# Second mixer of a two-model transformer kernel: attention and recurrence issued between the projections' matmuls

## The chip, the cores and the metric

The kernel runs on one core of a Trainium2 chip. TensorE (PE) does matrix products, its weight loads are listed apart (PEld); VectorE (DVE), ScalarE (ACT) and GpSimd (POOL) do elementwise work; SyncE (SP) issues most DMAs. Each engine runs its own instruction list in order and waits on semaphores. The metric is the device time of one execution, in microseconds (us).

## What is computed

Two models in a row, 512 tokens of width 1024, all in float32. In feature-major form an activation is 8 chunks of 128 features by 512 tokens. The order is: gated feed-forward, mixer (attention and pooling), gated feed-forward, final norm; then twice a mixer and a convolutional feed-forward. The change is in the first mixer of the second model, the `even_mixer` of the reference:

```python
def even_mixer(y, w_in, w_out, sinks, lb, gnorm_w):
    proj = y @ w_in                       # 1024 -> 2816: q, k, v, then q, f, i, g of HGRN
    qa, ka, va, qb, fb, ib, gb = jnp.split(proj, EVEN_SPLITS, axis=-1)
    # 8 query heads of 64 on 2 key heads, rotary; chunk attention over 128 tokens back, with sinks
    oa = chunk_band_attention(qa, ka, va, A_PREV_CHUNKS, None, sinks)
    ob = hgrn2(qb, fb, ib, gb, lb, gnorm_w)            # 4 heads, key and value width 128
    return jnp.concatenate([oa, ob], axis=-1) @ w_out

# hgrn2, over 16 blocks of 32 tokens: f = lb + (1 - lb) sigmoid(fb), k = 1 - f, cum = cumsum(log f)
#   q_dec = q exp(cum), k_dec = k exp(-cum), k_end = k exp(last - cum)
#   o_intra = causal(q_dec k_dec^T) v ;  o_inter = q_dec state
#   state   = exp(last) state + k_end^T v
#   o = rms_norm over the head's 128 values, times norm_w, times silu(gb)
```

## The kernel before

The network is a list `STAGES`: `up1 down1 in1 out1 up2 down2 in2 out2 up3 down3 in3 out3 up4 down4`. A product of a 128x128 weight tile with 512 tokens is done by `product` as three matmuls (high part times high part, high times low, low times high: L1135 to L1137), since each operand is split in a rounded part and a rest. I call these three a tile product. `in2` has 22 output chunks of 8 tile products (176), `out2` has 64.

Weights come in pairs of 16 tiles (1 MB) through two slots. SP loads `raw`, ACT rounds to `w_hi`, DVE subtracts to `w_lo` and releases the pair (`lo_rounded`), PE waits for that semaphore at the pair's start. In plain stages this is one 128x2048 instruction on each engine (L1337, L1370); in woven stages it is cut in four 128x512 pieces (`round_piece` L1352, `rest_piece` L1360), issued at every fourth tile product of the pair before; the last piece of a pair stands on DVE two tile products after it stands on ACT.

Two kinds of mixer code exist. `in1/out1` and `in3/out3` are woven: one loop over tile products g = 1, 2, ... on PE, ACT and DVE, and at fixed g each engine also issues a slot of attention (in `in1/out1` every third g). `in2/out2` is not woven. Its `in2` runs a pair at a time, with the two chunks of a pair interleaved, so that each chunk of the input `x_split` serves two tile products in a row; `hgrn_prepare_act` and `hgrn_prepare_dve` are called between pairs, and two `hgrn_transpose` stand between pairs on PE. Then `attention_pe/act/dve` run (8 heads by 4 query blocks, 32 units), then `hgrn_pe/act/dve` (4 heads), and then `out2`. In the HGRN part the output is made feature by token, so the sum of squares over a head's features is a matmul with ones (`mean_square`, L858), and the inverse root comes back through another (`spread_root`, L863). Its recurrence is 15 DVE instructions in a chain per head (L1043).

At the start of `in2`, ACT and DVE still make `x_split` chunk by chunk from the final norm of the first model (L1394, L1398), and PE waits for chunk k before it uses it. `mix_hi` and `mix_lo` are the split input of `out2`. `hg_kend` and the like are semaphores of the HGRN part.

## Time and profile before

| | us |
|---|---|
| median of 3 runs | 2252.61 |
| lowest and highest of them | 2243.70, 2253.09 |
| profiled execution | 2243.01 |
| its span in the trace | 2241.2 |
| PE busy in it | 2188.5 |
| DVE busy | 1169.6 |
| ACT busy | 716.9 |
| from the first tile product of in2 (901.48) to the end of out2's last (1199.34) | 297.86 |

PE is busy for 98% of the span by the page, but a busy PE is not a PE at full speed: a matmul's end is modelled, and the granted clock counts. The times between the starts of neighbouring matmuls tell more. DVE and ACT are far from full over the whole run; in a stage whose steps depend on them they may still be late.

### The profile page before, as it was taken

To read this page: it belongs to the slowest core of one execution; us is meant where nothing else is said; L and a number is where in the kernel's file an instruction comes from. 1 tells how busy PE (TensorE), PEld (TensorE's weight loads), DVE (VectorE), ACT (ScalarE), POOL (GpSimd) and SP (SyncE) were. 2 spreads that over 40 slices of the span, in tenths; PEclk is the share of its full clock that TensorE was granted. 3 is DMA by queue.
4 is the path that set the end of the run, shared out by engine and by line. 5 is a ranking of instruction groups with operands and counts; after the bars stand their busy time and mean duration, and the time that the engine had idled before them with its cause. 6 is when DMAs were issued, how large, how long until landed. Compare 5 with 4: busy or idle time off the path is not lost.

```text
span 2241.2 us, 26561 instructions
## 1 busy us (share of the span) xinstructions
PE 2188.5 (98%) x10146; PEld 1754.0 (78%) x10146; DVE 1169.6 (52%) x1777; ACT 716.9 (32%) x1012; POOL 119.7 (5%) x111
## 2 busy tenths in 40 slices
PE   8999999999999999999999999999899999999997
PEld 6888888677888888785687888888677777888886
DVE  4444434776444433744656666632655557666523
ACT  4222222354222222532313322222444444232221
POOL 0000000400000000000002000000411102000001
PEclk9999999999999999997979999999999999999998
DMA  7222234112222233221002222223222212222231
GB/s 251 94 98 106 68 103 155 62 43 90 98 106 96 71 100 123 81 94 57 1 11 69 91 100 106 77 89 113 79 75 95 76 60 80 105 94 94 77 103 64
DMA packets 32880, 198.99 MB, mean 89 GB/s; under 512 B 3760, under 2 KB 4064, under 8 KB 16048
## 3 DMA queue, kind: packets, MB, share of 16 engines
q1 hardware_dynamic: 29664, 184.91, 23.8%
q0 software_dynamic: 2992, 12.97, 2.0%
q8 instruction: 40, 0.66, 0.1%
q10 hardware_dynamic: 160, 0.26, 0.0%
q14 instruction: 24, 0.20, 0.0%
HBM read 195.74 MB, written 7.38 MB: 91 GB/s over the span
## 4 chain that ended last, share of the span: by engine, by line
PE 93%; DVE 3%; POOL 1%; ACT 1%; issue 1%; DMA 0%; POOLq 0%; SPq 0%; DVEq 0%; ACTq 0%
PE ps L1135 28%; PE ps L1136 27%; PE ps L1137 27%; POOL h L1815 1%; PE ps L633 1%; PE ps L651 1%; PE ps L1115 1%; PE ps L430 1%; PE ps L899 1%; PE ps L622 1%; PE ps L450 1%; PE ps L742 1%; PE ps L1131 1%; PE ps L756 0%; ACT w_hi L1337 0%
## 5 line engine op out<-in xcount | busy, mean ns | idle before, releaser
L1135 PE MATMUL ps<-x_split,w_hi 128*128 128x512 f32 x1856 | 738.4, 398 | 19.5 <-DVE x_split L1398 13.7
L1136 PE MATMUL ps<-x_split,w_hi 128*128 128x512 f32 x1856 | 724.8, 391 | 0.0
L1137 PE MATMUL ps<-x_split,w_lo 128*128 128x512 f32 x1856 | 724.7, 390 | 0.0
L1337 ACT ACTIVATE w_hi<-raw 128x2048 fp32r<-128x2048 f32 (+2 forms) x169 | 289.2, 1711 | 602.5 <-PE ps L1137 597.2
L1370 DVE TENSOR_TENSOR w_lo<-raw,w_hi 128x2048 fp32r<-128x2048 f32 (+2 forms) x169 | 344.3, 2037 | 219.3 <-ACT w_hi L1337 218.8
L1135 PEld LDWEIGHTS ps<-x_split,w_hi 128*128 128x128 f32 x1856 | 349.5, 188 | 111.1 <-DVE x_split L1398 14.2
L1136 PEld LDWEIGHTS ps<-x_split,w_hi 128*128 128x128 f32 x1856 | 349.8, 188 | 73.3 <-issue 3.6
L1137 PEld LDWEIGHTS ps<-x_split,w_lo 128*128 128x128 f32 x1856 | 349.5, 188 | 73.7
L1135 PE MATMUL ps<-act,w_hi 128*128 128x512 f32 x896 | 353.5, 395 | 1.6 <-DVE w_lo L1360 1.5
L1137 PE MATMUL ps<-act,w_lo 128*128 128x512 f32 x896 | 349.7, 390 | 0.0
L1136 PE MATMUL ps<-act,w_hi 128*128 128x512 f32 x896 | 349.7, 390 | 0.0
L1135 PEld LDWEIGHTS ps<-act,w_hi 128*128 128x128 f32 x896 | 168.8, 188 | 41.4 <-issue 4.4
L1137 PEld LDWEIGHTS ps<-act,w_lo 128*128 128x128 f32 x896 | 168.6, 188 | 35.6
L1136 PEld LDWEIGHTS ps<-act,w_hi 128*128 128x128 f32 x896 | 168.8, 188 | 35.0 <-issue 0.8
L1694 DVE TENSOR_TENSOR gate<-ps,rstd 128x512 f32<-128x512 f32 x44 | 30.4, 691 | 174.2 <-PE ps L1137 174.2
L1514 ACT ACTIVATE act<-prod 128x512 f32 (+1 forms) x88 | 55.6, 632 | 202.4 <-DVE prod L1714 202.4
L1738 DVE TENSOR_TENSOR act<-prod,act 128x512 f32 (+1 forms) x88 | 60.9, 692 | 88.3 <-ACT act L1514 88.3
L1697 DVE TENSOR_TENSOR shifted<-ps,rstd 128x512 f32<-128x512 f32 x44 | 30.4, 692 | 105.4 <-PE ps L1137 105.3
L1496 ACT ACTIVATE gated<-gate 128x512 f32<-128x512 f32 x88 | 54.8, 623 | 93.1 <-DVE gate L1709 85.9
L1815 POOL TENSOR_TENSOR h<-h,gate 128x512 f32<-128x512 f32 x16 | 24.6, 1535 | 1116.4 <-DVE gate L1771 1116.4
L1360 DVE TENSOR_TENSOR w_lo<-raw,w_hi 128x512 fp32r<-128x512 f32 x92 | 68.9, 753 | 26.9 <-ACT w_hi L1352 26.7
L1374 ACT ACTIVATE sq<-y 128x512 f32<-128x512 f32 (+1 forms) x32 | 19.8, 631 | 149.8 <-DVE y L1728 143.9
(224 smaller groups left out, 1679.6 us busy)
## 6 DMA issues: line engine op xcount, KB each, us to landing
raw<-in_w_up SPq DMA_DIRECT2D x88, 1024.0 KB, 4.8
raw<-in_w_in SPq DMA_DIRECT2D x28, 1024.0 KB, 4.8
raw<-in_w_down SPq DMA_DIRECT2D x32, 768.0 KB, 4.2
raw<-in_w_down SPq DMA_DIRECT2D x32, 640.0 KB, 3.8
raw<-in_w_out SPq DMA_DIRECT2D x12, 1024.0 KB, 4.8
skew<-scratch POOLq DMA_DIRECT2D x1, 5120.0 KB, 30.4
biases<-skew POOLq DMA_DIRECT2D x16, 256.0 KB, 3.0
h<-in_x_t SPq DMA_DIRECT2D x4, 512.0 KB, 10.2
```

The source lines that it names most:

```text
L1135: pe.matmul(bank(b), hi, rhs_hi, start=start, stop=False)
L1136: pe.matmul(bank(b), hi, rhs_lo, start=False, stop=False)
L1137: return pe.matmul(bank(b), lo, rhs_hi, start=False, stop=stop)
L1337: eng.activation(w_hi[:, w], raw[:, w], ACT.Copy).then_inc(hi_rounded, 1)
L1360: ins = eng.tensor_tensor(w_lo[:, w], raw[:, w], w_hi[:, w].bitcast(F32), ALU.subtract)
L1370: eng.tensor_tensor(w_lo[:, w], raw[:, w], w_hi[:, w].bitcast(F32), ALU.subtract).then_inc(lo_rounded, 1)
L1496: eng.activation(gated[:, :], gate[:, :], ACT.Silu if st.evac == "silu" else ACT.Gelu)\
L1514: eng.activation(chunk(act, f), prod[:, :], ACT.Copy).then_inc(prod_hi, 1)
L1694: eng.tensor_tensor(gate[:, :], bank(b), rstd[:, :], ALU.mult).then_inc(gate_ready, 1)
L1697: eng.tensor_tensor(shifted[:, 2:], bank(b), rstd[:, :], ALU.mult).then_inc(u_ready, 1)
L1738: eng.tensor_tensor(chunk(act, KF + f), prod[:, :], chunk(act, f).bitcast(F32), ALU.subtract)\
L1815: eng.tensor_tensor(chunk(h, m), chunk(h, m), (gate, gated)[m % 2][:, :], ALU.add).then_inc(h_ready, 1)
```

## The change

`in2` and `out2` become woven stages, by the code of `in1/out1`, which now takes the layer number `a` (0 or 1). The 22 output chunks of `in2` are made one at a time ( in the order f, g, then i and q in turns, then key, query, query, value, query, query of attention). The first four chunks have banks of their own, as in `in3`, so that PE needs not wait for the norm's factor `rstd` early.

Attention of this layer uses the grouped code of `in1` (16 steps that take two heads together, every third g from g = 154 on, into `out2`), without the doubled key copy `kdup` and its selection matrices; the swapped key halves come by two DMAs that ACT issues at g = 143. HGRN stands at fixed g: preparation at g = 26 to 70, heads 0 to 3 at a distance of 16 g between g = 70 and 145. Its output is made token by feature: the query part is the stationary operand (32 columns), the state moves (128 columns), the sum of squares comes from ACT's accumulator, and a transpose brings the normed output back. `out2` takes its inputs in the order HGRN first, attention last, the first four of each sum for all eight chunks and then the last four, with `y` added up in two parts on DVE. Weights of `in2/out2` are rounded in pieces.

```diff
-    Stage("in2", "in", 11, 11, "project"), Stage("out2", "in", KD // 2, KD // 2, "hold"),
+    Stage("in2", "in", 11, 22, "weave"), Stage("out2", "in", KD // 2, 2 * KD, "weave_hold", first=4),
-IN2_ORDER = [*range(10, 14), *range(6, 10), *range(18, 22), *range(14, 18), *range(0, 6)]
+IN2_ORDER = [*range(10, 14), *range(18, 22), 14, 6, 15, 7, 16, 8, 17, 9, 4, 0, 1, 5, 2, 3]
...
+        def hgrn_pe(pe, g):
+            hd, e = divmod(g - 64, 2 * KD)
+            if 0 <= hd < 4 and e == 6:
+                pe.wait_ge(hg_kend, 1)
...
+                    ins = pe.transpose(bank(O_BANK)[:, n * P:(n + 1) * P], chunk(hf, hd)[:, n * P:(n + 1) * P], ident)
...
+            if 0 <= hd < 4 and e == 11:
+                pe.wait_ge(evacuated, BY["in2"].g0 + 2 * hd + 9)
+                pe.wait_ge(hg_tb, hd + 1)
+                if hd:
+                    pe.wait_ge(hg_on, hd)
...
+            if 0 <= hd < 4 and e == 14:
+                pe.wait_ge(hg_ta, hd + 1)
...
+                    ins = pe.matmul(bank(UPDATE_BANKS[r])[:, n * P:(n + 1) * P], hf[rows, w], hv[rows, w], start=True, stop=True)
...
+            hd, e = divmod(g - 80, 2 * KD)
+            if 0 <= hd < 4 and e == 3:
+                pe.wait_ge(hg_q, hd + 1)
...
+            if 0 <= hd < 4 and e == 8:
                 pe.wait_ge(hg_s, hd + 1)
+                pe.wait_ge(hg_state, (NHB - 1) * (hd + 1))
...
+                            ins = pe.matmul(bank(O_BANK)[32 * r:32 * r + 32, n * P:(n + 1) * P],
+                                            chunk(hq, hd)[:, b * HGRN_BLOCK:(b + 1) * HGRN_BLOCK], state[hd % 2][:, state_col(b)],
+                                            start=False, stop=True, skip_group_check=True)
                 ins.then_inc(hg_o, 1)
...
+            if 0 <= hd < 4 and e == 13:
+                pe.wait_ge(hg_on, hd + 1)
...
+        def hgrn_act(eng, g):
...
+            if g == 43:
                 eng.wait_ge(hg_f, 2)
                 eng.activation(hf, hf, ACT.Ln).then_inc(hg_ln, 1)
+            if g == 59:
+                eng.wait_ge(hg_cum, 1)
+                eng.activation(he[:, :], hc[:, :], ACT.Exp).then_inc(hg_exp, 1)
                 eng.wait_ge(hg_diff, 1)
                 eng.activation(hf, hf, ACT.Exp).then_inc(hg_exp, 1)
+                eng.wait_ge(hg_exp, 1)
                 eng.activation(hc[:, :], hc[:, :], ACT.Exp, scale=-1.0).then_inc(hg_exp, 1)
...
+            hd, e = divmod(g - 80, 2 * KD)
+            if 0 <= hd < 4 and e == 9:
                 eng.wait_ge(hg_o, hd + 1)
+                for n in range(NB):
+                    w = slice(n * P, (n + 1) * P)
+                    ins = eng.activation(o_sq[:, w], bank(O_BANK)[:, w], ACT.Square, accum_out=h_sum[:, n:n + 1])
+                ins.then_inc(hg_osq, 1)
+                eng.wait_ge(hg_osq, hd + 1)
+                eng.activation(h_std, h_sum, ACT.Sqrt, bias=lbs[:, 31:32], scale=1.0 / P).then_inc(hg_std, 1)
...
+        def hgrn_dve(eng, g, link):
...
+            for hd in range(4):
+                at_ = 64 + 2 * KD * hd
+                if g in (at_ + 15, at_ + 17):
...
+                    for b in range(8) if g == at_ + 15 else range(8, NHB - 1):
...
+            hd, e = divmod(g - 80, 2 * KD)
+            if 0 <= hd < 4 and e == 0:
+                eng.wait_ge(evacuated, BY["in2"].g0 + 2 * hd + 10)
+                eng.tensor_tensor(chunk(hq, hd), chunk(hq, hd), chunk(he, hd), ALU.mult).then_inc(hg_q, 1)
...
+            if 0 <= hd < 4 and e == 11:
+                eng.wait_ge(hg_std, hd + 1)
+                link(eng.reciprocal(h_inv, h_std))
...
-            def in1_pe(pe, st):
+            def weave_pe(pe, st, a):
+                end = KD * st.groups
+                own = {2: TURN_BANK, 3: TURN_BANK + 1} if a else {}
+                mean_at, spread_at = ((6, 9), (2 * KD + 2, 3 * KD))[a]
...
+                    if a == 1:
+                        hgrn_pe(pe, g)
```

What stands in a row on ACT, where the exponentials of the preparation are. `w_hi<-raw` is the rounding of weights, `hc` holds the running sums, `he` their exponentials. Before:

```order
L921 ACT_TABLE_LOAD
L921 ACTIVATE proj<-proj 128x2048 [waits hg_diff]
L922 ACTIVATE he<-hc 128x2048
L924 ACTIVATE hc<-hc 128x2048 [waits hg_exp]
L1337 ACTIVATE w_hi<-raw 128x2048 [waits pair_done,raw_landed1]
```

After (g = 48 to 68):

```order
L1156 ACTIVATE w_hi<-raw 128x512 [waits pair_done,raw_landed1]
L1156 ACTIVATE w_hi<-raw 128x512 x2
L745 ACT_TABLE_LOAD
L745 ACTIVATE he<-hc 128x2048 [waits hg_cum]
L747 ACTIVATE proj<-proj 128x2048 [waits hg_diff]
L749 ACTIVATE hc<-hc 128x2048 [waits hg_exp]
L1156 ACTIVATE w_hi<-raw 128x512
L1156 ACTIVATE w_hi<-raw 128x512 [waits pair_done,raw_landed0]
L752 ACT_TABLE_LOAD
L752 ACTIVATE proj<-proj 128x2048 [waits evacuated]
```

The fourth piece of a pair's rounding, which the tile product g = 65 needs, now stands behind the three exponentials.

On PE, the recurrent part of one HGRN head, before (L889 and L899 make the output of head 0, then the updates of head 1 and the sum of squares):

```order
L868 MATMUL ps<-proj,hc 128x128 x4
L899 MATMUL ps<-proj,state_98 128x32 [waits hg_state] x15
L876 MATMUL ps<-proj 128x128 x15
L858 MATMUL ps<-small,osq 128x1 [waits hg_osq]
L858 MATMUL ps<-small,osq 128x1 x3
```

After, from g = 88 to 93 (L951 to L953 are the tile product):

```order
L716 MATMUL ps<-proj,sq 128x128 [waits hg_tb,hg_state,hg_s]
L716 MATMUL ps<-proj,sq 128x128 x3
L722 MATMUL ps<-state_88,proj 32x128 x15
L951 MATMUL ps<-x_split,w_hi 128x512 [waits evacuated]
...
L688 MATMUL ps<-small,proj 128x128 [waits hg_on,hg_tb,evacuated]
L688 MATMUL ps<-small,proj 128x128 x3
...
L729 MATMUL ps<-small,gate 128x128 [waits hg_on]
L729 MATMUL ps<-small,gate 128x128 x3
```

There are three tile products between the head's output (L722) and the transposes (L688), which wait for the normed output of this head, and two more before L729.

On DVE, the same head, before and after (`w_lo<-raw` is the weight rest; L1400 takes a projection chunk out of PSUM):

```order
L1040 COPY state0_98<-ps 128x128 [waits hg_u_ps]
L1043 SCALAR_TENSOR_TENSOR state0_98<-state0_98,tiny_66,ps 128x128 [waits hg_state] x14
L1005 COPY_PREDICATED s_t_100<-mconst_68,ps 128x512 [waits hg_s_ps]
```

```order
L832 COPY state0_88<-ps 128x128 [waits hg_u_ps]
L835 SCALAR_TENSOR_TENSOR state0_88<-state0_88,tiny_66,ps 128x128 [waits hg_state] x7
L1400 TENSOR_TENSOR proj_67<-ps,rstd_62 128x512 [waits pair_done]
L840 TENSOR_TENSOR proj_67<-proj_67,he_86 128x512 [waits evacuated]
L835 SCALAR_TENSOR_TENSOR state0_88<-state0_88,tiny_66,ps 128x128 [waits hg_state] x7
L1164 TENSOR_TENSOR w_lo_54<-raw_52,w_hi_53 128x512 [waits hi_piece]
L848 COPY_PREDICATED sq_60<-mconst_68,ps 128x512 [waits hg_s_ps,const_landed]
```

The chain of states is now cut in two, with a chunk's eviction and the query product (L840) between the halves.

## Rows read from the trace of the kernel before

**Rows 1.** Windows (start:end length, busy of PE, PEld, DVE, ACT, POOL, PEclk, DMA, GB/s).

```profile
901.48:1029.46 127.98, 125.95 (x572) 103.66 (x571) 72.45 (x67) 49.40 (x42) 0.00 (x0) 1.00 0.25 91
1029.46:1103.76 74.30, 66.29 (x252) 35.46 (x253) 46.13 (x183) 31.56 (x103) 0.00 (x0) 0.82 0.04 15
1103.76:1153.00 49.24, 46.82 (x344) 42.34 (x345) 35.59 (x85) 6.33 (x12) 0.00 (x0) 0.70 0.00 1
1153.00:1199.34 46.34, 46.34 (x194) 37.75 (x193) 18.21 (x20) 9.52 (x10) 0.00 (x0) 0.95 0.20 68
```

**Rows 2.** Timeline of PE in out2 (start, us, instruction).

```profile
1159.20 0.39 PE L1135 MATMUL ps<-act,w_hi 128*128 128x512 f32 x1
1159.43 0.40 PE L1136 MATMUL ps<-act,w_hi 128*128 128x512 f32 x1
```

**Rows 3.** Timeline of PE, one attention slot of in1.

```profile
444.30 0.82 PE L730 MATMUL ps<-small,g_exps 128*128 128x128 f32 x6
445.04 0.48 PE L742 MATMUL ps<-proj 64*128 64x256 f32 x1
...
445.68 0.88 PE L756 MATMUL ps<-g_turned,g_vtok 128*64 128x128 f32 x12
446.48 0.50 PE L1135 MATMUL ps<-x_split,w_hi 128*128 128x512 f32 x1
446.82 0.39 PE L1136 MATMUL ps<-x_split,w_hi 128*128 128x512 f32 x1
```

**Rows 4.** Timeline of PE, one rotary slot of in1.

```profile
452.34 1.02 PE L815 MATMUL ps<-proj,mconst 128*128 128x512 f32 x2
452.80 0.80 PE L1135 MATMUL ps<-x_split,w_hi 128*128 128x512 f32 x1
```

**Rows 5.** Timeline of PE, transposes and first HGRN products of in2.

```profile
970.01 1.91 PE L848 MATMUL ps<-small,proj 128*128 128x128 f32 x16
971.67 0.48 PE L1135 MATMUL ps<-x_split,w_hi 128*128 128x512 f32 x1
...
1103.76 1.16 PE L868 MATMUL ps<-proj,hc 128*128 128x128 f32 x8 [1.41 <-DVE act L531]
1104.85 1.17 PE L876 MATMUL ps<-proj 32*128 32x128 f32 x30
1105.94 1.16 PE L889 MATMUL ps<-s_t,proj 128*128 128x128 f32 x8
```

**Rows 6.** Timeline of DVE: last chunk of x_split before in2.

```profile
909.70 0.75 DVE L1398 SCALAR_TENSOR_TENSOR x_split<-h,vec,x_split 128x512 fp32r<-128x512 f32 x1 [0.38 <-ACT x_split L1394]
```

**Rows 7.** Timeline of ACT in in2.

```profile
929.24 1.28 ACT L915 ACT_TABLE_LOAD   x1
930.53 1.92 ACT L915 ACTIVATE hk<-proj 128x2048 f32<-128x2048 f32 x1
```

**Rows 8.** Groups of DVE, 905 to 1203.3 (count | busy us, mean ns | idle before).

```profile
L1043 DVE SCALAR_TENSOR_TENSOR state<-state,tiny,ps 128x128 f32<-128x128 f32 x56 | 19.5, 348 | 1.9
L975 DVE TENSOR_TENSOR_SCAN hc<-reset,proj 128x512 f32<-128x512 f32 x4 | 4.6, 1206 | 0.9 <-ACT proj L918 0.9
L979 DVE TENSOR_TENSOR proj<-hc 128x2048 f32<-128x2048 f32 x1 | 2.3, 2292 | 0.0
```

**Rows 9.** Groups of DVE, weight pieces in in1 and out1.

```profile
L1360 DVE TENSOR_TENSOR w_lo<-raw,w_hi 128x512 fp32r<-128x512 f32 x32 | 27.1, 853 | 3.4 <-ACT w_hi L1352 3.4
```

**Rows 10.** Groups of ACT, 905 to 1203.3.

```profile
L478 ACT ACTIVATE near<-near,tiny 128x129 f32<-128x129 f32 x4 | 1.6, 403 | 6.8 <-DVE tiny L524 6.8
L478 ACT ACTIVATION_READ_ACCUMULATOR near<-near,tiny 128x1 f32 x18 | 3.4, 188 | 0.0
```

**Rows 11.** Windows: PE thinly used, with its clock.

```profile
403.00:409.00 6.00, 4.83 (x19) 3.12 (x18) 5.97 (x6) 1.84 (x3) 5.59 (x5) 1.00 0.14 30
1040.00:1066.00 26.00, 26.00 (x66) 12.95 (x64) 12.30 (x59) 8.96 (x32) 0.00 (x0) 0.50 0.00 0
1592.00:1600.00 8.00, 5.82 (x18) 4.37 (x19) 7.02 (x7) 4.39 (x7) 3.58 (x4) 0.79 0.17 44
```

760 lines of the change are left out of this document (272 added, 488 removed).

## The prediction

> **What bounds the kernel now.** I read the windows of the stretch that the change touches first, then the starts of neighbouring matmuls on PE, then who waits for whom. Over the whole run PE never rests long, and nearly all of its time is weight tile products. At full clock two matmuls start 0.23 us apart (1159.20, 1159.43) [rows 2], so a tile product of three costs 0.683 us. In the stretch from the first tile product of in2 to the end of out2's last, 901.48 to 1199.34 or 297.86 us, there are 240 of them, which is 163.9 us. The rest, 134 us, is work of another kind, and the windows say where it lies [rows 1]: in2 takes 127.98 for 176 tile products (120.2), so it is almost tight; attention takes 74.30 us and HGRN 49.24 us in which no tile product runs, at a mean clock of 0.82 and 0.70; out2 takes 46.34 for 43.7, since its first tile products run at half clock. In the two middle windows DVE is busy 62% and 72% and ACT 42% and 13%. So neither is full there: PE, DVE and ACT wait for each other in chains of small steps, and the halved clock makes PE's small steps long. What PE does in these 123.5 us is little work. That is what a weave can hide.
>
> **PE's work in the new stretch.** (1) 240 tile products, 163.9 us. (2) Statistics of the norm, as now: two small groups and the tile product after each, about 1.9 us, the same before. (3) Attention: 16 steps. A slot of in1 shows the parts [rows 3]: six transposes take 0.74 (444.30 to 445.04), scores of 256 keys for two heads 0.64 (to 445.68), twelve value passes 0.80 (to 446.48), and the next matmul comes 0.34 instead of 0.23 after the first, which is 0.11 for coming back. With this layer's window a step reads two key blocks (four transposes, eight passes, 256 keys: 0.49 + 0.64 + 0.53 + 0.11 = 1.8), and in the first query block of each of the four head pairs one (about 1.05, with 0.4 taken for scores of 128). 12 x 1.8 + 4 x 1.05 = 25.8 us; say 26. (4) Five rotary products: 0.46 each (452.34 to 452.80), and the first matmul after one is 0.80 long where 0.39 is usual, so 0.9 each, 4.5 us [rows 4]. The transposes of v: 0.5. (5) HGRN, per head: three groups of four transposes at 1.66 / 4 = 0.42 (970.01 to 971.67 for sixteen), scores 1.09, updates 1.09, the part within a block about 1.0 [rows 5], and the part with the state. This last has no row: before, the state was the stationary operand and 32 columns moved; now 32 columns are stationary and 128 move, with 15 products in four groups of array columns. The nearest rows are the updates, which use a quarter of the rows each and take 1.09 for 30 passes [rows 5], and the value passes of attention, which use half of the columns by turns and take 0.067 each, so 2.0 for 30 [rows 3]. Without any overlap it would be 1.09 / 8 = 0.136 for a pass, 4.1 us for 30. I take 1.1, since four groups follow one another as in the updates; the other end adds 3.0 x 4 = 12 us. A head is 3 x 0.42 + 1.09 + 1.09 + 1.0 + 1.1 = 5.5, with six returns at 0.11 it is 6.2, four heads 24.8 us. Together PE has 163.9 + 1.9 + 26 + 4.5 + 0.5 + 24.8 = 221.6 us of work at full clock.
>
> The Trainium skill (TensorEngine Tiling (Array Packing), Key Properties) says that changing the tiling mode drains TensorE, which speaks against small matmuls strewn among large ones. It gives no time. The slot above holds such changes in both directions and its 2.18 us include them, so the sum would be the same by the rule.
>
> **PE's waits in the new stretch.** These I follow through the order of each engine, with g for the tile product at which a step stands.
>
> - Start. PE waits for input chunk k before tile product k. In the old order a chunk served two tile products, now one, so PE runs up to the producer. DVE ends the eighth chunk at 910.45 (909.70 + 0.75) [rows 6], and g = 8 ends at 911.2 where it would end at 906.9: 4.3 us lost.
> - g = 33. DVE waits for the norm's factor, then does four weight pieces, three evictions and four tiny steps, 4 x 0.75 to 0.85 + 3 x 0.69 + 0.9 = 6.2 or more from some 0.6 + 0.7 after PE's spread; PE needs the fourth piece after 0.4 + 8 x 0.683 = 5.9. About 1.3 us [rows 9].
> - g = 65. The preparation is a chain: sigmoid on ACT, f and k on DVE (3.4, four of 128x512 at 0.54 and one of 128x2048 at 1.23 in the same view as rows 8), logarithm on ACT, four scans on DVE (1.21 each), difference (2.29), exponentials on ACT; a 2048-wide step on ACT is 1.92 and a table load ahead of it 1.28 [rows 7, 8]. From the end of g = 32 at 929.5 I get: sigmoid done 933.5, f and k 937.1, logarithm 939.1, scans 948.2 with three weight pieces and an eviction among them, difference 952.1 (two more in front), exponentials 950.2, 954.1, 956.0. The fourth piece of the rounding stands behind them on ACT, 956.7, and its rest on DVE ends at 957.5. PE has finished g = 64 at 952.6 and waits 4.8 us. Queued behind that wait on PE is everything; on DVE the eviction of g = 64 and k_end.
> - Each head, g = +3: the query product on DVE stands behind eight state steps (2.9 with 0.35 each and small gaps [rows 8]), and an eviction. PE reaches the scores 2.05 us after it finished the pair, the product is there after 3.1. 1.0 us each, 4 us.
> - Each head, g = +11: after the head's output ACT squares four blocks with the accumulator. The nearest rows are exponentials of 129 columns, 0.40 + 0.19 for the read [rows 10], 2.4 us for four; then root 0.26, DVE reciprocal and product 0.9, with semaphores 3.7. PE has three tile products to do, 2.05 us, before the next head's transposes wait for this. 1.65 us for three heads, 5 us, and 1.3 once for the table load of the root [rows 7]. The last head has no such transposes.
> - Attention. The slots of in1 follow each other at 4.3 us for wider steps with hardly a gap, and DVE's load per slot is smaller here; 1 us.
>
> That is 4.3 + 1.3 + 4.8 + 4 + 5 + 1.3 + 1 = 21.7 us. DVE in a head has about 13 us of work in 20, so it is not the bound; ACT less. Weight pieces take DVE 4 x 0.75 for a pair where one instruction took 2.29, hidden in that slack, save at the three places above. SP's loads move nothing: 1 MB per pair, released at the same tile product as now. The constants' DMA of POOL is 3/4 as long and lands before g = 100. The end of out2 with its norm is as in out3, a few tenths either way.
>
> **The clock.** At half clock a tile product costs twice. In3 starts with the same hunger for input chunks, and its window 1592 to 1600 has a clock of 0.79: 1.7 us at half, 0.9 us lost. At 403 to 409 PE was busy 80% with a gap of 1.2, and the clock stayed at 1.00. From 1040 to 1066, after gaps and with thin work, it was 0.50 throughout [rows 11]. After the wait at g = 65 the clock may fall and come back under dense work, as in out2, whose window is 2.6 us over its 43.7 [rows 1]. I take 2.5 us for both.
>
> ACT's table loads: in the trace the work after a load begins at once, 929.24 + 1.28 against 930.53 [rows 7]. The Trainium skill (ScalarE: Activation LUTs, What ACT_TABLE_LOAD costs) gives about 1.38 us of drain on top of 1.28. By that rule the chain to g = 65 would be 2 x 1.38 longer, and the sum 3 us higher; the trace does not agree, and I leave it out.
>
> **The sum.** 221.6 + 21.7 + 2.5 = 245.8 us against 297.9, a gain of 52.1 us. On the profiled execution's own time, 2243.0, this gives 2190.9. The median of the three runs is 2252.6, which is 9.6 above the profiled execution; one of the three ran like it, 2243.7. I carry the same distance over: 2200 us, about 2.3% faster.
>
> **Rivals.**
> (a) PE's work and fewer waits: the chains at g = +3 and +11 are shorter than I count (squares at 0.35 each), and the wait at g = 65 is half as long. Gain 60 to 68, 2185 to 2193. For it: in1 and out1 have almost no waits on PE. Against: HGRN's chain has three more engine changes for a head than attention's.
> (b) Longer waits or slower state products: no overlap of the column groups (+12), or the clock falls at each head's waits and half of the HGRN stretch of some 78 us runs at half level, which adds 0.9 us (0.68 and the small work with it) for each of about 25 of its g, 20 us. Gain 20 to 40, 2213 to 2233. For it: HGRN before ran at 0.70. Against: there PE had only small matmuls, and here 11 of 20 us are dense.
> (c) Slower than before: the clock, once fallen at g = 65, stays at half to the end of the weave, because the waits of every head keep PE too thin, as in 1040 to 1066 [rows 11]. Each g from 65 on then costs 0.68 and its small work again, about 0.9 us. From some 58 g's on (52 / 0.9) the gain is gone; the 111 that remain of in2 with the part of out2 up to its slots would cost 100, 2300 us. Against it: out2 came back to full clock within about 5 us of tile products alone. The Trainium skill (TensorE: Matmul & The Clock Gate, HAM oscillation) tells of a kernel whose waits bring the clock down again and again; here the rows with a gap of 1.2 us show none.
> (d) The weave doesn't do what it says, since a semaphore makes PE stand at the first HGRN slot until the preparation is over and the rest runs as before: the order gives PE tile products on both sides of each slot, so only a small chance; no change, 2252.
>
> **Chances.** The forecast 0.55 (2193 to 2208), (a) 0.17, (b) 0.23, (c) 0.03, (d) 0.02. The likeliest time is 2200. The range leaves out (c), (d) and the far part of (b): 2183 to 2224. A measurement of this kernel tells about 0.5% (11 us) from no change; faster by more has 0.96, within it 0.02, slower by more 0.02.
>
> **What would show it.** In the profile after: no stretch without tile products between in2 and out2; the two starts 246 us apart (235 to 270); on PE a wait for `w_lo` of about 5 us some 56 us after in2's start; a wait for `x_split` at the start of 4 us in small parts; waits of 1 to 2 us for `gate` (the normed output) three times, and four of about 1 us for the query product; the state products at 1.1 us for 30 passes; the clock near 1.00 everywhere but at the start and after g = 65. The forecast is wrong if the clock row shows half level across the heads, if the state products take 4 us, or if DVE is busy without a break in the heads, which would mean that its chains and not PE's work set the pace.

## The result and the profile after

The changed kernel takes 2185.24 us (median of 4 runs, 2185.03 to 2185.57) where the kernel before takes 2252.85 (4 runs, 2243.70 to 2260.18). The ratio is 0.9719, interval 0.9685 to 0.9753. The forecast was 2200 in a range of 2183 to 2224, so the direction and the range hold; the time lies 2 us above the range's low end, below the forecast's own 2193 to 2208 and at the fast end of rival (a), 2185 to 2193. In the groups of runs below, two of the 27 runs of the kernel before took 3223.7 and 3113.4 us at a mean granted clock of 0.63 and 0.65; the ratios leave them out.

The page of the profiled execution (2185.57 us) shows PE where it was in share, with less time in all, and no slice at a low clock:

```profile
span 2183.6 us, 26539 instructions
PE 2132.3 (98%) x10116; PEld 1709.3 (78%) x10116; DVE 1164.7 (53%) x1810; ACT 726.3 (33%) x1071; POOL 119.9 (5%) x111
PEclk9999999999999999999999999999999999999999
```

The stretch from in2's first tile product to the end of out2's last takes 239.77 us (902.39 to 1142.16) where it took 297.86. Outside the stretch next to nothing moved: 1943.34 us before, 1943.83 after. The windows (start:end length, busy of PE, PEld, DVE, ACT, POOL, PEclk, DMA, GB/s) are the whole stretch, the piece after the wait at g = 65, and the HGRN heads:

```profile
902.39:1142.16 239.77, 227.99 (x1331) 173.70 (x1329) 167.53 (x389) 105.39 (x225) 0.00 (x0) 0.99 0.18 63
956.45:962.28 5.83, 5.83 (x19) 4.57 (x20) 5.80 (x6) 3.47 (x3) 0.00 (x0) 0.71 0.56 183
962.28:1041.60 79.32, 73.88 (x569) 58.66 (x567) 51.66 (x112) 23.54 (x66) 0.00 (x0) 1.00 0.16 54
```

The two windows at clocks 0.82 and 0.70 [rows 1] have no counterpart. The heads now share 79.32 us with 71 tile products at full clock, and DVE is busy 65% of it: its load doesn't set the pace there, but the order of its steps still makes PE wait, as the next lines show.

What PE still waits for in the stretch, but for one wait of 0.2 us (engine, line waited for: us in total, times, longest):

```profile
PE ps L951 <- DVE w_lo L1164: 3.8, 2, 3.4
PE ps L707 <- DVE proj L840: 3.1, 4, 0.8
PE ps L688 <- DVE gate L855: 2.4, 3, 1.6
PE ps L951 <- DVE x_split L1202: 2.2, 6, 0.8
```

These are the four kinds that the prediction named: the weight piece at g = 65, the query product, the normed output, and the input chunks. The timeline rows (start, us, instruction, idle before it) show each. First PE at g = 64 and 65, then a row after it, then ACT and DVE beside it:

```profile
952.70 0.39 PE L953 MATMUL ps<-x_split,w_lo 128*128 128x512 f32 x1
956.45 0.50 PE L951 MATMUL ps<-x_split,w_hi 128*128 128x512 f32 x1 [3.36 <-DVE w_lo L1164]
...
959.31 0.63 PE L951 MATMUL ps<-x_split,w_hi 128*128 128x512 f32 x1
959.74 0.63 PE L952 MATMUL ps<-x_split,w_hi 128*128 128x512 f32 x1
```

```profile
953.26 1.89 ACT L749 ACTIVATE hc<-hc 128x2048 f32<-128x2048 f32 x1
955.06 1.13 ACT L1156 ACTIVATE w_hi<-raw 128x512 fp32r<-128x512 f32 x2
```

```profile
955.70 0.69 DVE L1164 TENSOR_TENSOR w_lo<-raw,w_hi 128x512 fp32r<-128x512 f32 x1 [3.69 <-ACT w_hi L1156]
```

ACT's weight piece stands behind its exponentials, the last of which ends at 955.15; DVE's piece waits for it, and PE for DVE. From 958.03 to 961.02 matmuls start 0.43 apart (959.31 to 959.74) where it is 0.23 at full clock. The granted clock is at its half level from 957.83 to 961.25, 3.4 us, and that costs 1.7 us against the full level.

Then PE in the first head:

```profile
974.36 1.16 PE L707 MATMUL ps<-proj,hc 128*128 128x128 f32 x8 [0.78 <-DVE proj L840]
...
979.27 1.05 PE L716 MATMUL ps<-proj,sq 128*128 128x128 f32 x8
980.25 1.07 PE L722 MATMUL ps<-state,proj 128*32 128x128 f32 x30
981.25 0.50 PE L951 MATMUL ps<-x_split,w_hi 128*128 128x512 f32 x1
...
985.22 0.63 PE L688 MATMUL ps<-small,proj 128*128 128x128 f32 x4 [1.64 <-DVE gate L855]
```

And ACT behind the output (981.25 on):

```profile
981.38 0.28 ACT L765 ACTIVATE prod<-ps 128x128 f32<-128x128 f32 x1 [2.19 <-PE ps L722]
981.55 0.19 ACT L765 ACTIVATION_READ_ACCUMULATOR prod<-ps 128x1 f32 x1
...
982.54 1.28 ACT L768 ACT_TABLE_LOAD   x1
983.84 0.30 ACT L768 ACTIVATE tiny<-tiny,lbs 128x4 f32<-128x4 f32 x1
```

The 15 state products, 30 passes on PE, take 1.00 us (980.25 to 981.25), near the forecast's value of 1.1 and not at its other end. The four squares with their reads take 1.16 us (981.38 to 982.54), not 2.4: the next square follows after 0.25 to 0.27 us, since a square and its read overlap.

### The profile page after: what moved, and what is told of

It is laid out like the page before. It is cut to its first block, busy times and chain, and to the rows that moved or that the text cites. A ratio compares the mean times of both kernels' runs of the same rounds, so it can differ in the third digit from the quotient of the medians.

```text
span 2183.6 us, 26539 instructions
## 1 busy us (share of the span) xinstructions
PE 2132.3 (98%) x10116; PEld 1709.3 (78%) x10116; DVE 1164.7 (53%) x1810; ACT 726.3 (33%) x1071; POOL 119.9 (5%) x111
## 4 chain that ended last, share of the span: by engine, by line
PE 92%; DVE 4%; ACT 2%; POOL 1%; issue 1%; DMA 0%; POOLq 0%; SPq 0%; DVEq 0%
PE ps L951 28%; PE ps L953 27%; PE ps L952 27%; POOL h L1629 1%; PE ps L449 1%; PE ps L467 1%; PE ps L565 1%; PE ps L931 1%; PE ps L579 1%; PE ps L438 1%; PE ps L553 1%; ACT x_split L1198 1%; DVE w_lo L1164 1%; PE ps L947 1%; ACT w_hi L1141 1%
## 5 line engine op out<-in xcount | busy, mean ns | idle before, releaser
L951 PE MATMUL ps<-x_split,w_hi 128*128 128x512 f32 x1856 | 744.4, 401 | 25.3 <-DVE x_split L1202 16.3
L953 PE MATMUL ps<-x_split,w_lo 128*128 128x512 f32 x1856 | 725.9, 391 | 0.0
L951 PEld LDWEIGHTS ps<-x_split,w_hi 128*128 128x128 f32 x1856 | 349.9, 189 | 122.8 <-DVE x_split L1202 19.4
L1141 ACT ACTIVATE w_hi<-raw 128x2048 fp32r<-128x2048 f32 (+2 forms) x155 | 262.4, 1693 | 531.0 <-PE ps L953 522.4
L1174 DVE TENSOR_TENSOR w_lo<-raw,w_hi 128x2048 fp32r<-128x2048 f32 (+2 forms) x155 | 312.3, 2015 | 211.9 <-ACT w_hi L1141 211.5
L953 PEld LDWEIGHTS ps<-x_split,w_lo 128*128 128x128 f32 x1856 | 350.0, 189 | 74.5
L951 PE MATMUL ps<-act,w_hi 128*128 128x512 f32 x896 | 353.4, 394 | 1.8 <-DVE w_lo L1164 1.5
L953 PE MATMUL ps<-act,w_lo 128*128 128x512 f32 x896 | 349.0, 390 | 0.0
L951 PEld LDWEIGHTS ps<-act,w_hi 128*128 128x128 f32 x896 | 168.1, 188 | 43.0 <-issue 6.6
L953 PEld LDWEIGHTS ps<-act,w_lo 128*128 128x128 f32 x896 | 168.2, 188 | 35.6
L1164 DVE TENSOR_TENSOR w_lo<-raw,w_hi 128x512 fp32r<-128x512 f32 x148 | 107.5, 730 | 36.8 <-ACT w_hi L1156 36.5
L1156 ACT ACTIVATE w_hi<-raw 128x512 fp32r<-128x512 f32 x148 | 88.5, 620 | 68.9 <-PE ps L953 68.7
```

The source lines that it names most:

```text
L951: pe.matmul(bank(b), hi, rhs_hi, start=start, stop=False)
L953: return pe.matmul(bank(b), lo, rhs_hi, start=False, stop=stop)
L1141: eng.activation(w_hi[:, w], raw[:, w], ACT.Copy).then_inc(hi_rounded, 1)
L1156: eng.activation(w_hi[:, w], raw[:, w], ACT.Copy).then_inc(hi_piece, 1)
L1164: ins = eng.tensor_tensor(w_lo[:, w], raw[:, w], w_hi[:, w].bitcast(F32), ALU.subtract)
L1174: eng.tensor_tensor(w_lo[:, w], raw[:, w], w_hi[:, w].bitcast(F32), ALU.subtract).then_inc(lo_rounded, 1)
```

## The experiments

Runs of one changed kernel lie up to 7 us apart (e2_start), so for each kernel I give the median and, from its trace, the length of the stretch and the mean clock of the window 930 to 965, which holds the wait at g = 65. Each group of runs had its own runs of the kernel before, with medians of 2246.7, 2251.9 and 2251.0 us; the yardstick `e0_after` and 3, 7 and 8 ran in the second group, 1, 2, 4 and 9 in the first, 5, 6, 10 and 11 in the third. A median can move a little more than its stretch, because short pieces at the half clock outside the stretch also come and go: outside it the profile of the changed kernel has 1943.8 us, those of e0_after, e1_piece, e9_all and e10_best 1942.4, 1942.2, 1941.4 and 1943.2.

| kernel | median, us | stretch, us | clock, 930 to 965 |
|---|---|---|---|
| before | 2252.85 | 297.86 | |
| after | 2185.24 | 239.77 | 0.95 |
| e0_after (the same again) | 2185.16 | 240.88 | 0.90 |
| e1_piece | 2178.73 | 234.47 | 1.00 |
| e2_start | 2186.64 | 241.94 | 0.95 |
| e3_cols | 2190.38 | 244.34 | 0.95 |
| e4_states | 2183.34 | 237.23 | 1.00 |
| e5_late | 2181.23 | 236.32 | 1.00 |
| e6_table | 2183.74 | 239.56 | 0.90 |
| e7_hburst | 2228.09 | 283.24 | 0.90 |
| e8_aburst | 2198.61 | 252.58 | 0.95 |
| e9_all | 2175.70 | 230.54 | 1.00 |
| e10_best | 2175.24 | 230.07 | 1.00 |
| e11_both | 2241.16 | 297.73 | 0.90 |

**The yardstick.**

> The changed kernel itself once more, as the yardstick for the runs beside it. Both theories: 2185 us within 3 us; whether its runs scatter by 0.5 us (as in its first 4) or by several us shows how far single runs may be read.

Its four runs lie between 2184.61 and 2185.37. The stretch is 1.1 us longer than in the first profile, with more of it at the half clock; so a single stretch is good to 1 to 2 us as long as the wait at g = 65 is there (e4_states and e5_late have it and no half clock, 1.6 us less). Where I name less than that, it is read from the places in the trace that the edit touches.

### What the placing is worth

**HGRN in one burst.** The slots are undone, the work is not:

```diff
                     if a == 1:
-                        hgrn_pe(pe, g)
+                    if a == 1 and g == 129:
+                        for gg in range(64, 147):
+                            hgrn_pe(pe, gg)
```

and alike for ACT (steps from g = 67 on) and DVE (from g = 71 on).

> The changed kernel with all TensorE steps of the four HGRN heads, and the ScalarE and VectorE steps from the first state on, in one burst behind the tile product at g = 129, in place of slots between the tile products; the attention slots stay where they are. No computation is left out. Theory (the gain comes from tile products that fill TensorE's waits for ScalarE and VectorE): a head alone is the chain of transposes, copies, updates, 15 state steps of 0.38 us, scores, mask, intra and state products, squares, roots, normalising and transposing back, some 12 to 15 us with 6.2 us of TensorE work in it; 4 heads with little overlap give 4 x 6 = 24 us of waits and in them the half clock for part of it, 2200 to 2215 us, with a scatter between runs as the kernel before has. Rival (the serial stretch of before was slow for its order of heads and its start, and a burst costs next to nothing): under 2192 us.

Measured: 2228.09 us (2227.55 to 2231.07), the stretch 43.5 longer. The direction is the theory's, the size is beyond its upper end, and the scatter is 3.5 us, not that of the kernel before. The burst's window and its first head on PE:

```profile
1004.44:1074.78 70.34, 38.01 (x354) 31.66 (x352) 32.98 (x83) 13.91 (x49) 0.00 (x0) 0.62 0.00 1
```

```profile
1007.13 1.17 PE L698 MATMUL ps<-proj 32*128 32x128 f32 x30 [0.69 <-ACT proj L759]
1011.99 2.08 PE L707 MATMUL ps<-proj,hc 128*128 128x128 f32 x8 [3.69 <-DVE proj L840]
...
1023.50 1.09 PE L688 MATMUL ps<-small,proj 128*128 128x128 f32 x4 [3.89 <-DVE gate L855]
```

Four heads take 70.3 us. PE is idle for 32.3 of them (I had estimated 24 for all waits), behind the chain of states (3.69) and the normalising (3.89) of each head; and it is busy for 38.0 because the clock has fallen to 0.62. In the slots of the changed kernel the same heads take 30 us: 5.4 idle, and 24.6 for the work and for coming back to tile products. So the burst itself costs 40.3 more, 26.9 of idle time and 13.4 of busy time. The other 3.3 are half clock in tile products: 2.2 in those behind the burst and 1.1 at g = 65, where this execution stayed at the half level longer. The half clock stood in the expectation without a price of its own; it is about two fifths of the cost (13.4 and 3.3 of 43.5).

**Attention in one burst.** The 20 slots and the last rotary step stand between in2 and out2:

```diff
             def slot_at(a, g):
+            if a == 1:
+                return -1
...
+                if a == 1:
+                    rope_pe(pe, a, ROPED[a][-1])
+                    for i in range(20):
+                        grouped_pe(pe, a, i)
```

> The changed kernel with the 20 attention slots and the last rotary step of the second layer in one burst between the projection and the output projection, in place of slots between tile products; the HGRN steps stay woven. No computation is left out. Theory (each slot's 1.5 to 1.8 us of products is followed by a wait for exponentials, products and sums on ScalarE and VectorE that only tile products can fill): 20 slots of some 1 us more, 15 to 25 us and the half clock in part of them, 2200 to 2210 us. Rival (slots of neighbouring groups already fill each other's waits): under 2190 us.

Measured: 2198.61 us, the stretch 12.8 longer; a little less than the theory's 15 to 25. The burst:

```profile
1068.56:1111.22 42.66, 31.98 (x236) 17.99 (x235) 30.37 (x151) 27.01 (x85) 0.00 (x0) 0.92 0.07 24
```

PE is busy for 75% of this burst against 54% of the HGRN one, and the clock holds better (0.92 against 0.62). The slots of neighbouring steps fill each other's waits to a good part: what the rival said is half true. So attention gains 12.8 us from its placing and HGRN 43.5.

**Both.**

> The changed kernel with both bursts: the HGRN heads at g = 129 and the attention slots between the projection and the output projection. Nothing of the new code is left out, only the placing between tile products is undone. Single bursts cost 43.5 us (HGRN) and 12.8 us (attention) in the stretch. Theory (the two are independent): 239.8 + 43.5 + 12.8 = 296.1 us in the stretch, 2241 us in all, so that placing alone makes up the change's gain and the rewritten steps add next to nothing. Rival (in the kernel before the two parts follow each other and share the lowered clock, so together they cost more than apart): over 302 us, 2248 us or more. If runs of this one scatter by several us where the changed kernel scatters by 1, the scatter comes from the stretch at the lowered clock.

Measured: 2241.16 us and a stretch of 297.73, with 296.1 and 2241 expected. The two parts add up, and in the profiled stretch the new code without its placing takes what the old one took (297.73 and 297.86). Its median stays 0.5% below that of the kernel before (ratio 0.9953, interval 0.9925 to 0.9982), whose runs scatter upward. The windows, in order: in2 up to the burst, HGRN, the rest of in2, attention with the last rotary step, out2:

```profile
900.34:1001.41 101.07, 95.05 (x399) 75.28 (x398) 60.22 (x86) 42.66 (x56) 0.00 (x0) 0.97 0.24 83
1001.41:1071.90 70.49, 38.16 (x354) 31.82 (x352) 32.98 (x83) 13.93 (x49) 0.00 (x0) 0.64 0.00 1
1071.90:1110.08 38.18, 38.18 (x155) 29.74 (x153) 20.34 (x31) 7.18 (x13) 0.00 (x0) 0.94 0.21 64
1110.08:1154.19 44.11, 34.27 (x235) 19.72 (x234) 30.54 (x151) 27.19 (x85) 0.00 (x0) 0.85 0.07 24
1154.19:1198.07 43.88, 43.88 (x194) 36.35 (x193) 25.03 (x39) 13.20 (x23) 0.00 (x0) 0.99 0.21 72
```

That the sums agree is partly chance. Beside [rows 1], attention in a row takes 44.1 us where the old code took 74.3, and HGRN in a row 70.5 where the old took 49.2: the grouped attention is the better serial code, and the HGRN order, written for slots, the worse one. Between tile products this matters less, for there PE's own time counts and what is left of the waits. Why the old HGRN order is 21 us quicker in a row wasn't tried. Nor was the old attention code placed in slots: the bursts price the placing of the new code, and what placing would give the old one isn't shown.

### The state products

```diff
-                for n in range(NB):
-                    for r in range(4):
+                for r in range(4):
+                    for n in range(NB):
                         b = 4 * n + r
```

> The changed kernel with the HGRN state products ordered by column group first (8 or 7 products of the same 32 columns in a row) and not block by block (next to each other, four products of four different column groups). After the change the 8 intra products and these 30 together take 1.98 us in a slot. Theory (products of different column groups overlap, so that 30 take 1.1 us): in the new order they run one after another at the spacing of an ordinary product of 128 columns (0.11 to 0.14 us), some 4 us a head in place of 1.1, 4 x 3 = 12 us more and a little less where it fills a wait: 2195 to 2198 us. Rival (a product of 32 columns is simply short, 0.036 us, overlap or none): the same 1.98 us and 2185 us.

Measured: 2190.38 us, the stretch 4.6 longer; between the two. The same place as above on PE:

```profile
978.91 1.05 PE L716 MATMUL ps<-proj,sq 128*128 128x128 f32 x8
979.89 2.24 PE L722 MATMUL ps<-state,proj 128*32 128x128 f32 x30
982.07 0.50 PE L951 MATMUL ps<-x_split,w_hi 128*128 128x512 f32 x1
```

The 15 products take 2.18 us in place of 1.00, 1.2 us a head more, 4.7 for four. So the rival (the order doesn't matter) falls. The single records show why the price is not the theory's 3 us a head. These windows count the passes of L722 alone (length, PE busy, passes, clock); first the changed kernel, then e3_cols:

```profile
980.24:980.38 0.14, 0.13 (x4) 1.00 0.00 0
```

```profile
979.88:980.02 0.14, 0.13 (x1) 1.00 0.00 0
```

In the changed kernel four passes on four column groups start within 0.02 us (980.250 to 980.270), and the next four 0.11 later. In e3_cols passes on the same group start 0.11 us apart, as the theory had it; but the next group begins when the one before it is only about halfway (at 980.14, 980.61 and 981.07, where the first group's six passes start from 979.89 to 980.46), so about two groups run side by side. Mean spacing is 0.073 us there and 0.033 in the changed kernel, a factor of 2.2. A case with no overlap at all was not run, so the forecast's other end, 4.1 us a head, is not measured; even the order by groups stays 1.9 below it.

The Trainium skill (TensorE: Matmul & The Clock Gate, Part 3: Packing small matmuls) has products of different column groups run at the same time. By that the order of column groups matters, and the trace agrees: four starts within 0.02 us against one in 0.11.

### The waits, one by one

**The weight piece at g = 65.**

```diff
-            if g == 59:
+            if g == 61:
                 eng.wait_ge(hg_cum, 1)
                 eng.activation(he[:, :], hc[:, :], ACT.Exp).then_inc(hg_exp, 1)
```

> The changed kernel with ScalarE's HGRN exponentials moved two tile products later (from g = 59 to g = 61), so that they stand behind the weight piece that the tile product at g = 65 needs, not ahead of it. In the trace after the change TensorE waits 3.36 us at 956.45 for that piece and then runs at the half clock until 961.4, which costs about 1.7 us more. Theory (the wait at g = 65 is only ScalarE's order, and the half clock follows from it): both go, 3.4 + 1.7 = 5.1 us less than the changed kernel's 2185.2, 2180.1 us. Rival (the exponentials then delay the next thing in the row, the first products of head 0 or the next piece, by as much): the wait turns up behind 962, and the time is 2183 to 2185.5.

Measured: the stretch is 5.3 us shorter (5.1 expected), the median 2178.73, below the 2180.1 expected because this kernel's profile also has 1.6 us less outside the stretch. The wait at g = 65 is gone, nothing took its place (the 0.5 left of `w_lo` is the one at g = 33, and the other rows read as after), and the clock of the window 930 to 965 is 1.00:

```profile
PE ps L951 <- DVE w_lo L1164: 0.5, 1, 0.5
```

```profile
930.00:965.00 35.00, 34.53 (x181) 28.18 (x180) 26.74 (x34) 24.07 (x24) 0.00 (x0) 1.00 0.27 94
```

The same window of the yardstick:

```profile
930.00:965.00 35.00, 31.65 (x129) 25.60 (x128) 24.22 (x30) 22.33 (x21) 0.00 (x0) 0.90 0.26 90
```

Over all profiles, the three with bursts among them: of the ten with the wait of 3.4 us at this place, eight show the half clock after it and two (e4_states, e5_late) don't; of the three without the wait (e1_piece, e9_all, e10_best) none does. So the wait brings the clock down, but not in every execution.

**The start.**

```diff
                     j, k = divmod(g - 1, KD)
+                    if a == 1 and g <= 2 * KD:
+                        k, j = divmod(g - 1, 2)
```

> The changed kernel with the first tile products of the second layer's projection walked in pairs: each of the first contraction chunks serves both column tiles before the next chunk is needed. After the change TensorE waits 3.6 us in all over the first 8 tile products (902.39 to 911.41) because VectorE makes a chunk of x more slowly than TensorE uses it up. Theory (only the rate of chunks is short): two tile products to a chunk give each chunk 1.37 us of work, the gaps go, and the time falls by 3 to 3.6 us to about 2182. Rival (the second tile's weights come later than the x chunks and TensorE waits for them in their place): 2184 to 2187 us.

Measured: 2186.64 us (2182.66 to 2189.27), the stretch 2.2 longer. The time is the rival's, its reason isn't. The gaps for `x_split` are gone, and PE waits 2.69 us once, for something that neither side had named, the sum of squares of the norm:

```profile
917.09 1.84 PE L941 MATMUL ps<-small,ssum 128*128 128x1 f32 x8 [2.69 <-DVE ssum L1197]
```

```profile
909.73 0.75 DVE L1204 SCALAR_TENSOR_TENSOR x_split<-h,vec,x_split 128x512 fp32r<-128x512 f32 x1 [0.38 <-ACT x_split L1200]
910.40 2.29 DVE L1176 TENSOR_TENSOR w_lo<-raw,w_hi 128x2048 fp32r<-128x2048 f32 x1
912.61 3.54 DVE L1195 TENSOR_TENSOR squares<-squares 128x2048 f32<-128x2048 f32 x2
916.25 0.69 DVE L1197 TENSOR_TENSOR ssum<-squares 128x512 f32<-128x512 f32 x1
```

```profile
917.00:925.00 8.00, 7.91 (x25) 6.66 (x26) 2.59 (x8) 3.31 (x6) 0.00 (x0) 0.57 0.01 2
```

DVE works without a break from the chunks through a weight pair and the squares to the sum at 916.94. PE needs this sum at g = 18 in either order. With the gaps it came there 1.2 us after the sum, without them 2.7 before: the start is bound by DVE's list, and the gaps were the cover of a second wait. And one wait of 2.69 can be dearer than six with 2.2 in sum: here the clock falls after it (0.57 from 917 to 925), which it didn't in the changed kernel's start. In e9_all the same wait left it at 1.00, and there the paired start does gain: from the first tile product to the nineteenth 16.5 us, where the changed kernel takes 17.5. So the edit is worth 1.0 us at full clock and loses 2 when the clock falls.

**The query product.**

```diff
-                    for b in range(8) if g == at_ + 15 else range(8, NHB - 1):
+                    for b in range(4) if g == at_ + 15 else range(4, NHB - 1):
```

> The changed kernel with VectorE's chain of HGRN states cut after 4 blocks instead of 8, so that the query product that TensorE's score matmuls need stands four state steps earlier in VectorE's row. After the change each head's score matmuls wait, 3.1 us over the 4 heads, and each slot loses 0.97 us against its own work. Theory (the query product is late only because of the eight state steps ahead of it): the four waits go, 3 to 4 us less, 2181.5 to 2182 us. Rival (the eleven state steps left over delay the states that the state part's matmuls read): a wait on the states turns up in the slot after, and the time is 2184 to 2187 us.

Measured: 2183.34 us, the stretch 2.5 shorter, of which 1.6 is the half clock that this execution hadn't. What is left for the edit is 0.9: the four waits at L707 give back 4.1, the new ones take 3.2. PE's waits from 965 to 1042:

```profile
PE ps L716 <- DVE sq L848: 2.3, 3, 1.1
PE ps L688 <- DVE gate L855: 2.3, 3, 1.6
```

The four waits at L707 are gone, three at L716 stand in their place: the score mask on DVE now comes behind eleven state steps. The rival's kind was right (a later wait), not its object, which it took to be the states. A cut moves the wait along DVE's chain between a head's updates and its intra products.

**The normed output.**

```diff
-            if 0 <= hd < 4 and e == 11:
+            if 0 <= hd < 4 and e == 12:
                 pe.wait_ge(evacuated, BY["in2"].g0 + 2 * hd + 9)
```

(and ACT's copy of v's transposes at 13, not 12)

> The changed kernel with TensorE's transposes of v for the next HGRN head one tile product later, and ScalarE's copy of them one later. Theory (the normed output is late by less than one tile product for heads 2 and 3 and by more for head 1, where the root's table is loaded): the segments lose 0.5, 0.5 and 0.7 us of their waits, the stretch comes to 238.1 us where it was 239.8, the whole to 2183.5. Rival (ScalarE's copy and the updates behind it then come late as well): the waits turn up at the updates, 239.8 us or more.

Measured in two runs: 2181.23 us, the stretch 3.5 shorter, again without the half clock (1.6), so 1.8 for the edit where 1.7 was expected. The waits for the normed output fall from 2.4 us in three to 1.0 in one, as the theory says, and none comes at the updates.

**The root's table.**

```diff
                 eng.activation(hg, hg, ACT.Silu).then_inc(hg_sig, 1)
+                eng.activation(tiny[:, 252:253], lbs[:, 31:32], ACT.Sqrt)
```

> The changed kernel with a square root of one column on ScalarE right after the gate's Silu at g = 66, so that the table of the root is loaded there and not behind the squares of the first head. Theory A (nothing waits for ScalarE at g = 66 to 68): the first head's wait for the normed output shrinks by the load's 1.28 us, 238.5 us in the stretch. Theory B (seen with all edits together: the load holds up a weight piece and an eviction behind it on ScalarE, and TensorE waits 0.7 us for that at v's first transposes): a gain of 0.6 us or less, 239.2 us.

Measured in two runs: 2183.74 us. The waits for the normed output fall from 2.4 to 1.1 us, by the table load's 1.28, as in theory A; the stretch is 1.3 shorter than the yardstick's, which has the same clock of 0.90 in the window 930 to 965, and 0.2 shorter than the first profile's, which has 0.95. So far A. Theory B's wait shows only where the wait at g = 65 is gone, as in the next kernel.

**All together, twice.** The first version combines the five edits above:

> The edits on the waits of the woven stretch together: exponentials behind the weight piece, paired tile products at the start, the state chain cut at 4, the transposes of v in the HGRN part one tile product later (with ScalarE's copy one later), and a square root of one column ahead of time, so that its table is loaded before the first head's squares. Theory (every wait is the order of one engine's row, and none hides another): 5.1 + 3.3 + 3.5 + 1.7 and up to 0.5 more = about 13.5 us less, 2171.5 us. Rival (some of the waits share a cause, and one that goes lengthens the next): 2176 to 2180 us.

Measured: 2175.70 us, the stretch 9.2 shorter, not 13.5: just below the rival's times, 4 above the theory's. The start gave 1.0 of its 3.3 and the cut at 4 gave 0.9 of its 3.5, as above. And the early table load holds up ACT's weight piece, DVE's rest of it starts only at 957.75 after a wait of 2.09, and v's eviction behind that on DVE is late at g = 76:

```profile
959.10 0.66 PE L688 MATMUL ps<-small,proj 128*128 128x128 f32 x4 [0.66 <-DVE proj L1403]
```

The second leaves the start as in the changed kernel, cuts the states at 6 and loads the table at g = 78:

```diff
+            if g == 78:
+                eng.activation(tiny[:, 252:253], lbs[:, 31:32], ACT.Sqrt)
...
-                    for b in range(8) if g == at_ + 15 else range(8, NHB - 1):
+                    for b in range(6) if g == at_ + 15 else range(6, NHB - 1):
```

> A version from what the runs so far showed: the exponentials behind the weight piece, the state chain cut after 6 blocks (after 8 the query product is late by 0.97 us a head, after 4 the mask of the scores by 0.75), the transposes of v one tile product later, and the root's table loaded at g = 78, where ScalarE has nothing pending, not at g = 66, where it held up a weight piece; the start as in the changed kernel. Theory (VectorE's chain between the updates and the intra products is about as long as the tile products beside it, so a cut in the middle leaves some 0.4 us of wait a head): 5.3 + 4 x 0.5 + 1.8 + 2 x 0.5 = 10 us less in the stretch, 229.7 us there and 2175 us in all. Rival (VectorE's load is what counts, and any cut loses the same 0.75 to 1 us a head): 231.7 us, 2177 us.

Measured: 2175.24 us (2175.09 to 2176.20), the stretch 230.07, with 2175 and 229.7 expected. It has the lowest median, 0.966 of the kernel before (interval 0.961 to 0.971) and 10 us below the changed one; e9_all, 0.5 above it with runs from 2173.95 to 2178.26, can't be told from it. This version with the paired start was not run. What PE still waits for in its stretch:

```profile
PE ps L953 <- DVE x_split L1204: 2.2, 6, 0.8
PE ps L716 <- DVE sq L850: 0.6, 1, 0.6
PE ps L953 <- DVE w_lo L1166: 0.5, 1, 0.5
PE ps L953 <- DVE prod L651: 0.2, 1, 0.2
```

## Why the prediction was right, and where it was off

Its chain of reasons holds: the two serial windows were mostly idle time, half clock and small matmuls taken a few at a time, and tile products fill them. The clock alone took 28 of their 123.5 us (0.18 of 74.3 and 0.30 of 49.2). And attention has the same passes before and after: 112 for the values, 56 transposes, 64 for the scores. PE was busy for 66 us of that window before (the rotary products among them), and the slots take 28.4. The value passes, first before, then in the slots (count | busy us, mean ns | idle before):

```profile
L450 PE MATMUL ps<-prob_t,v_tok 128*64 128x128 f32 x112 | 21.8, 319 | 2.4 <-ACT prob_t L470 2.4
```

```profile
L579 PE MATMUL ps<-g_turned,g_vtok 128*64 128x128 f32 x112 | 9.6, 287 | 0.0
```

Undoing the placing alone (e11_both) gives the whole gain in the stretch back, 58 us, and 56 of the 66 us between the medians. But by time it is rival (a) that came, and by mechanism a good part of it: the squares are quick, as it said (0.29 each with 0.35 named), and the wait at g = 65 is 3.4, shorter though not by half; the chain at g = +3 is as long as the forecast had it. That the range held, by 2 us, is partly luck, since two errors, 6.6 us in the waits and 9.6 in the last step, both made the forecast too slow. Against the trace of after its terms stand so:

| term | forecast, us | measured, us |
|---|---|---|
| 240 tile products | 163.9 | 163.9 |
| attention slots | 26 | 28.4 |
| HGRN, four heads | 24.8 | 23.1 |
| rotary, statistics, v transposes | 6.9 | 6.7 |
| wait at the start | 4.3 | 4.2 |
| g = 33 | 1.3 | 0.5 |
| g = 65 | 4.8 | 3.4 |
| query product, four | 4.0 | 3.9 |
| normed output, three, with the table load | 6.3 | 2.9 |
| attention waits | 1.0 | 0.2 |
| half clock | 2.5 | 1.7 |
| sum of the stretch | 245.8 | 239.8 |

(The measured terms are segments of PE's timeline less their tile products at 0.683; 0.8 us of small gaps is in none of them. A wait is counted here with what it costs its segment, so it is a little longer than the idle time in the lines above.)

- PE's work was right to 1 us in 221, with two errors that cancel: a head's transposes take 0.35 a group and not 0.42, its scores 0.91 and not the 1.09 of [rows 5], while attention stands in 19 slots where I counted 16 steps, and takes 2.4 more.
- The one term with an open price, the state products, was taken at the right end: 1.00 us for 30 passes, with 1.1 assumed. The nearest row (the updates) was a guess about column groups and not a measurement of them; e3_cols shows that the overlap is real.
- The waits were named one by one at the right places, 15.1 us of them where I summed 21.7. The step that was mis-sized most is the normed output: I took 0.59 us for a square with its read, from exponentials that the trace shows in a chain with other steps [rows 10], and added them up. In a row they overlap, 0.29 each on average; four cost 1.16. That alone is 1.2 us of the chain three times, and 3.4 in the sum.
- At g = 65 the forecast put the end of ACT's last exponential at 956.0, and the trace has it at 955.15, from a chain of a dozen steps. The order was right, so the remedy (e1_piece) followed from it, and it gave 5.3 us.
- The clock: half level for 3.4 us after the wait at g = 65, full everywhere else, nearly as forecast; the start, which the forecast thought might lose some too, stayed at 1.00. The row that priced it was misread: a mean clock of 0.79 over the 8 us from 1592 to 1600 [rows 11] is 3.4 us at half level and 1.7 lost, not 1.7 and 0.9. Rival (b)'s half clock in the heads and rival (c) didn't come: the seven waits of 0.4 to 1.6 us between tile products left it at 1.00 (window 962.28 to 1041.60).
- What was wrong is the last step, from the profiled execution to the median. The sum gives 2190.9 on the profiled execution's own time, and the stretch's 6 us less give 2185; I then added 9.6 us because the median of before lies that much above its profile. But this distance belongs to the part that the change removes. The runs of the kernel before go with their mean granted clock: in the third group from 2241.3 us at 0.984 over 2251.2 at 0.978 to 2264.9 at 0.970. With HGRN and attention in bursts (e11_both) ten runs spread over 5.6 us (2238.3 to 2243.9, clock 0.981 to 0.979), with the same code in slots (e0_after) four runs over 0.8, all at 0.994. The bursts bring back a part of the spread, not the 24 us of the kernel before; what makes the rest (its older serial code has more small steps at the low clock) was not isolated. Without the carry-over the point forecast would have been off by 5.7 us, not by 14.8.

## What to carry to other kernels

In this kernel a stage of small dependent steps cost its waits and, on top, the clock that they bring down; strewn between large matmuls it cost TensorE's own time for it and a small rest of the waits (5.4 us idle for the four HGRN heads, where the burst had 32), although its order was the slower one in a row. To forecast such a weave, sum TensorE's work from rows of like slots and then walk through each other engine's list for the things TensorE needs next; a place where a long step stands ahead of a weight piece is the first to look for. Carry the scatter of the old runs over only if the part that makes it remains, and before closing a gap, ask what has been waiting behind it.

## What the runs showed of the hardware

- 15 products with 32 stationary and 128 moving columns, 30 passes, take 1.00 us when neighbouring products use different column groups and 2.18 when they use the same (e3_cols). Passes on one group start 0.11 us apart; passes on four groups start within 0.02 us of each other.
- After one wait of 3.4 us among dense tile products the granted clock was at its half level for 3 to 6 us in eight executions of ten; after one of 2.69 us in one (e2_start) of two (e9_all not). In the kernel before, the half level in the window 1592 to 1600 comes with a wait of 1.96 us (PE at 1595.14). The waits of up to 1.6 us in the heads never did it in the woven profiles.
- A square with accumulator and its read (0.28 and 0.19 us) are followed by the next square after 0.25 to 0.27 us; four with their reads take 1.16 (981.38 to 982.54).
- Coming back from small matmuls to a tile product costs 0.11 us (the row at 981.25: the first matmul behind the state products is 0.50 long where 0.39 is usual), and 0.12 to 0.13 behind attention's value passes. So strewing small matmuls is nearly free: 0.12 to 0.13 in a slot's distance of 3.7 us.
